# A two-layer decoder trunk with split fp32 weights: slabs of the turned products prepared in pairs

## The chip, the cores and the metric

The kernel runs on one core of a Trainium2 chip. The metric is the device time of one execution in microseconds, as the median of several runs. Busy times, waits and orders come from one profiled execution, whose own time stands beside its span below.

## The reference

```python
DEPTH = 2; D_MODEL = 2048; SEQ = 256; D_FF = 5632; CONV_WIDTH = 3
for layer in range(DEPTH):
    h = rmsnorm(x, g_mix_pre[layer])
    y = even_mixer(...) if layer % 2 == 0 else odd_mixer(...)   # h @ w_in -> q, k, v -> attention -> @ w_out
    x = x + rmsnorm(y, g_mix_post[layer])
    h = rmsnorm(x, g_mem_pre[layer])
    y = memory_cross_attention(h, rmsnorm(mem, g_mem_kv[layer]), wq, wk, wv, wo)
    x = x + rmsnorm(y, g_mem_post[layer])
    h = rmsnorm(x, g_ffn_pre[layer])
    y = conv_ffn(h, w_up[layer], conv_w[layer], conv_b[layer], w_down[layer])
    x = x + rmsnorm(y, g_ffn_post[layer])

def conv_ffn(h, w_up, conv_w, conv_b, w_down):
    u = h @ w_up                                   # (256, 2048) @ (2048, 2 * 5632)
    u = conv_b + conv_w[0]*up[:, 0:S] + conv_w[1]*up[:, 1:S+1] + conv_w[2]*up[:, 2:S+2]
    g, val = u[..., :D_FF], u[..., D_FF:]
    return (silu(g) * val) @ w_down
```

Everything is float32. The weight products (`h @ w_in`, `h @ w_up` and so on) are nearly all of the work.

## The kernel before

**Split weights.** A weight matrix comes in slabs: 256 rows by 512 columns, which on chip is 128 partitions by 1024 elements (two k-tiles of 512 columns), 512 KB. SyncE loads slab n into `raw[:, n % 8]` (`slab`, L529 to L537). ScalarE rounds it to its high part, `w_hi[:, n % 4] = raw` (`split`, L636 to L642). VectorE then writes the low part, `w_lo = raw - w_hi` (L1350 to L1354); `w_lo` lies in the same memory as `raw`, so the low part overwrites the slab in place. TensorE multiplies with both parts. The activations are split in the same way into `a_hi` and `a_lo`, which stand side by side in `a_hl`.

**Four counters order this.** `raw_landed[s]` says that a slot's load has landed, `hi_ready` and `lo_ready` count high and low parts, and `slab_used` counts the slabs that TensorE has finished. SyncE issues slab n once `slab_used` is at least n - 7, ScalarE overwrites a slot of `w_hi` once `slab_used` is at least n - 3, and TensorE starts slab n once `lo_ready` is at least n + 1.

**Turned slabs.** In the query and key groups (groups 1 to 7 of each layer) and in all but the first group of `up`, TensorE keeps the weights stationary (`slab_turned`, L2319 to L2349). A slab then has 8 "wide" products with the high part (L2331; 512 columns, `a_hi` and `a_lo` together) and 8 "narrow" ones with the low part (L2339; 256 columns). Even slabs go wide then narrow, odd slabs narrow then wide, so TensorE changes between the two kinds once per slab. A group is 8 slabs (GS) into four PSUM banks.

**Who runs ahead.** ScalarE and VectorE each have one queue with an order written out by hand. In step s of a group they do that step's other work and then call `ahead`, which splits slab n + 2. The step's other work in `up` belongs to the group that was just finished. For a "val" group, with q counted from the start of the group that follows it: q = 0 ScalarE copies half of each bank to `u_val` (L1200), q = 1 VectorE adds the other half (L2020), q = 2 VectorE scales (L2027), q = 3 ScalarE does the first tap of the convolution in four instructions (L1215) and VectorE the other two taps in eight (L2037, L2045), q = 4 VectorE multiplies by the gate (L2068), q = 5 the result is split too (L1235, L2087). For a "gate" group it is the same from q = 8 to q = 11, with the SiLU at q = 12 (L1223). A pair of groups, 16 slabs, is one turn of `up_pair`. Turns 1 to 4 are written out; turns 5 to 10 are a loop (`Fori`), where the values that are waited for come from registers. Turn 0 has its own first half.

```python
def ahead(n, s=None):
    ...
    split(n + AHEAD, (n + AHEAD) % RAW if s is None else (s + AHEAD) % RAW)   # AHEAD = 2
```

Of the kernel before, what the change touches and what calls it, by code (L numbers as in the profile page):

```python
# [30 lines left out]
F32 = mybir.dt.float32  # L31
F32R = mybir.dt.float32r
I32 = mybir.dt.int32
ALU = mybir.AluOpType
# [3 lines left out]
P = 128  # L38
D = 2048
SEQ = 256  # L40
# [8 lines left out]
N = 512  # L49
# [94 lines left out]
def build(nc, x, mem, positions, w_in_ab, w_out_ab, w_in_c, b_f, w_out_c,  # L144
# [6 lines left out]
    with ctx:  # L151
# [273 lines left out]


        def pair_heads(q):

            return (2 * q, 2 * q + 1) if 0 <= q < HEADS // 2 else ()
# [98 lines left out]
        def _(sp):  # L528
            def slab(n, s, src):  # L529
# [15 lines left out]
            def groups_loop(n0, w, count, col0, stride, slabs, pair=1):  # L545

                with sp.Fori(0, count) as i:
                    for g in range(pair):
                        for s in range(slabs):
                            k = g * slabs + s  # L550
                            slab(i * (pair * slabs) + (n0 + k), k % RAW,
                                 w[s * SLAB_KT * P:(s + 1) * SLAB_KT * P, bass.ds(i * stride + (col0 + g * N), N)])

            sp.dma_start(raw[:, 0, 0, :], w_in_ab[0][0:P, 0:N]).then_inc(first_w[0], 16)
            w_ins, w_outs = (w_in_ab[0], w_in_c[0]), (w_out_ab[0], w_out_c[0])
            for L in range(LAYERS):
# [54 lines left out]
                with sp.Fori(0, FF_GROUPS) as i:  # L611
                    for g in range(2):
                        for s in range(GS):
                            k = g * GS + s
                            slab(i * (2 * GS) + (n0 + PHASE["up"] + k), k % RAW,
                                 w_up[L][s * SLAB_KT * P:(s + 1) * SLAB_KT * P, bass.ds(i * N + g * D_FF, N)])
                for k, (q, g, _) in enumerate(DOWN):
# [17 lines left out]
        def _(act):  # L635
            def split(n, s):  # L636


                act.wait_ge(raw_landed[s], landed(n, s))
                if not (isinstance(n, int) and n < RING):  # L640
                    act.wait_ge(slab_used, n - (RING - 1))
                act.activation(w_hi[:, s % RING], raw[:, s], ACT.Copy).then_inc(hi_ready, 1)  # L642

            def landed(n, s):
                if isinstance(n, int):
                    return landed_ahead[s] + 16 * (n // RAW + 1)
# [153 lines left out]
            for L in range(LAYERS):  # L800
# [63 lines left out]
                def qk_group(G, par, n):  # L864

                    turned = G != 1
                    for s in range(GS):
                        if s == 0 and turned:
                            qk_copy(G - 1, 1 - par)
# [21 lines left out]
                        mem_step((G - 3) * GS + s)  # L891
                        ahead(n + s, s)

# [455 lines left out]
        def _(dve):  # L1349
            def split(n, s):  # L1350


                dve.wait_ge(hi_ready, n + 1)
                dve.tensor_tensor(w_lo[:, s], raw[:, s], w_hi[:, s % RING].bitcast(F32), ALU.subtract).then_inc(lo_ready, 1)  # L1354

            def ahead(n, s=None):
# [154 lines left out]
            for L in range(LAYERS):  # L1511
# [99 lines left out]
                def qk_group(G, par, n):  # L1611
                    turned = G != 1
                    for s in range(GS):
                        if s == 0 and not turned:
                            qk_evac(G - 1, 1 - par)
# [15 lines left out]
                        mem_step((G - 3) * GS + s)  # L1631
                        ahead(n + s, s)

# [457 lines left out]
                def up_pair(i, n, first):  # L2091
                    for q in range(GS if first else 0, 2 * GS):
                        if not first:
                            val_tail(i - 1, q)
# [11 lines left out]
                        if q == GS + (4 if first else 3):  # L2106
                            conv_taps(i * 2, u_turned if first else lambda j: u_gate[:, j, :], conv_gate, 0, i)
                        ahead(n + q, q)

# [179 lines left out]
        def _(pe):  # L2289
# [31 lines left out]
            def slab_turned(n, slot, par, k0):  # L2321
# [27 lines left out]
                last.then_inc(slab_used, 1)  # L2349

            def transposes(dst, src, tiles, done):

# [93 lines left out]
            for L in range(LAYERS):  # L2446
# [58 lines left out]
                def qk_group_turned(G, par, n):  # L2505
                    qk_free(G)
                    for s in range(GS):
# [8 lines left out]
                        if L and G == 5 and s == 0:  # L2516
                            pe.wait_ge(*LV(L, "fg_st", 5))
                        slab_turned(n + s, s % RAW, par, SLAB_KT * s)

# [281 lines left out]
                def up_pair(i, n, first):  # L2801
                    for q in range(GS if first else 0, 2 * GS):
# [4 lines left out]
                        if first and q == GS + 3:  # L2807
                            u_turn()
                        slab_turned(n + q, q % RAW, q // GS, SLAB_KT * (q % GS))

# [126 lines left out]
```

## Time and profile before

| What | Value |
|---|---|
| Median of 3 runs | 2434.69 us (2433.88 to 2435.66) |
| Profiled execution, its own time | 2432.51 us |
| Span of the profiled execution | 2430.7 us |
| TensorE busy | 2415.9 us, 99% of the span |
| VectorE busy | 1855.5 us, 76% |
| ScalarE busy | 1369.8 us, 56% |
| GpSimd busy | 61.7 us, 3% |
| Mean TensorE clock granted | 0.999 of full speed |
| DMA | 477.85 MB, 197 GB/s over the span |

The own time is 1.8 us over the span, which runs from the first to the last instruction. TensorE's matmuls overlap in the records (each is shown longer than the distance to the next), so a busy share of 99% says that TensorE had nearly no gaps, and its pace is read from the distance between starts.

### The profile page before, as it was taken

How to read it: one execution, taken by the hardware profiler on the slowest of the kernel's cores; microseconds unless marked ns; L12 is line 12 of the kernel's file. 1: busy time of each engine (PE TensorE's matmuls, PEld its weight loads, DVE VectorE, ACT ScalarE, POOL GpSimd, SP SyncE). 2: the span in 40 equal slices, each digit the busy share in tenths (PEclk: the TensorE clock that was granted, in tenths of full speed). 3: DMA queues.
4: the chain of work that ended last, by engine and by line, in shares of the span. 5: the costliest groups of instructions: out<-in, count | busy, mean ns of one | idle time of the engine just before them, and what ended most of it. 6: DMA issues, size and time to landing. Idle time of an engine off the chain costs nothing.

```text
span 2430.7 us, 34866 instructions
## 1 busy us (share of the span) xinstructions
PE 2415.9 (99%) x12548; PEld 2067.8 (85%) x12548; DVE 1855.5 (76%) x2559; ACT 1369.8 (56%) x1960; POOL 61.7 (3%) x108
## 2 busy tenths in 40 slices
PE   9999999999999999999999999999999999999998
PEld 7888888888888888888888888888888888888887
DVE  7768877677777677888876588776776776778887
ACT  6545665665555555555555456656655555555554
POOL 0100000000000000000000003000000000000000
PEclk9999999999999999999999999999999999999999
DMA  8766556576666666666776665565666666666665
GB/s 309 250 196 202 163 161 188 164 217 190 190 191 188 187 188 189 208 207 210 228 209 184 191 202 184 164 188 172 210 190 190 191 189 187 187 189 212 203 214 184
DMA packets 252094, 477.85 MB, mean 197 GB/s; under 512 B 18256, under 2 KB 21472, under 8 KB 251968
## 3 DMA queue, kind: packets, MB, share of 16 engines
q1 hardware_dynamic: 234640, 447.83, 60.7%
q10 hardware_dynamic: 17328, 28.35, 3.7%
q8 instruction: 79, 1.29, 0.2%
q14 instruction: 47, 0.39, 0.1%
HBM read 468.89 MB, written 6.31 MB: 195 GB/s over the span
## 4 chain that ended last, share of the span: by engine, by line
PE 94%; DVE 2%; ACT 1%; DMA 1%; issue 1%; POOL 0%; ACTq 0%; POOLq 0%; DVEq 0%
PE acc L2331 17%; PE aux L2331 9%; PE acc L2339 9%; PE tp L2331 8%; PE acc L2310 7%; PE acc L2312 7%; PE acc L2311 7%; PE acc L2304 5%; PE acc L2306 5%; PE acc L2305 5%; PE aux L2339 5%; PE tp L2339 4%; PE tp L2310 1%; DVE w_lo L1354 1%; PE aux L2310 1%; PE aux L2312 1%
## 5 line engine op out<-in xcount | busy, mean ns | idle before, releaser
L1354 DVE TENSOR_TENSOR w_lo<-raw,w_hi 128x1024 fp32r<-128x1024 f32 x847 | 1016.8, 1222 | 425.3 <-ACT w_hi L642 422.6
L642 ACT ACTIVATE w_hi<-raw 128x1024 fp32r<-128x1024 f32 x847 | 867.2, 1054 | 363.4 <-DVE raw L2130 99.9
L2331 PE MATMUL acc<-a_hl,w_hi 128*128 128x512 f32 x1792 | 556.1, 392 | 0.9 <-DVE rope_sin L1568 0.9
L2331 PEld LDWEIGHTS acc<-a_hl,w_hi 128*128 128x128 f32 x1792 | 322.0, 189 | 55.4 <-issue 1.5
L2339 PE MATMUL acc<-a_hl,w_lo 128*128 128x256 f32 x1792 | 360.1, 283 | 0.5 <-DVE w_lo L1354 0.5
L2339 PEld LDWEIGHTS acc<-a_hl,w_lo 128*128 128x128 f32 x1792 | 293.6, 191 | 18.2 <-DVE w_lo L1354 0.8
L2331 PE MATMUL aux<-a_hl,w_hi 128*128 128x512 f32 x960 | 296.4, 390 | 0.0
L2331 PE MATMUL tp<-a_hl,w_hi 128*128 128x512 f32 x832 | 257.0, 390 | 0.0
L2331 PEld LDWEIGHTS aux<-a_hl,w_hi 128*128 128x128 f32 x960 | 180.2, 188 | 39.3
L2339 PE MATMUL aux<-a_hl,w_lo 128*128 128x256 f32 x960 | 193.4, 283 | 0.0
L2304 PE MATMUL acc<-w_hi,a_hl 128*128 128x512 f32 x476 | 191.1, 402 | 1.9 <-DVE a_hl L1383 1.1
L2306 PE MATMUL acc<-w_hi,a_hl 128*128 128x512 f32 x476 | 186.1, 391 | 0.0
L2305 PE MATMUL acc<-w_lo,a_hl 128*128 128x512 f32 x476 | 185.5, 390 | 0.0
L2331 PEld LDWEIGHTS tp<-a_hl,w_hi 128*128 128x128 f32 x832 | 156.2, 188 | 34.1
L2312 PE MATMUL acc<-w_hi,hid_lo 128*128 128x512 f32 x448 | 174.3, 389 | 0.0
L2339 PE MATMUL tp<-a_hl,w_lo 128*128 128x256 f32 x832 | 167.6, 283 | 0.0
L2310 PE MATMUL acc<-w_hi,hid_hi 128*128 128x512 f32 x416 | 161.8, 389 | 0.0
L2311 PE MATMUL acc<-w_lo,hid_hi 128*128 128x512 f32 x416 | 161.8, 389 | 0.0
L2339 PEld LDWEIGHTS aux<-a_hl,w_lo 128*128 128x128 f32 x960 | 149.3, 191 | 0.0
L2339 PEld LDWEIGHTS tp<-a_hl,w_lo 128*128 128x128 f32 x832 | 129.4, 191 | 0.0
L2304 PEld LDWEIGHTS acc<-w_hi,a_hl 128*128 128x128 f32 x476 | 89.4, 188 | 20.7 <-issue 2.0
L2306 PEld LDWEIGHTS acc<-w_hi,a_hl 128*128 128x128 f32 x476 | 89.3, 188 | 19.5
(382 smaller groups left out, 3266.8 us busy)
## 6 DMA issues: line engine op xcount, KB each, us to landing
raw<-in_w_up SPq DMA_DIRECT2D x352, 512.0 KB, 3.7
raw<-in_w_down SPq DMA_DIRECT2D x176, 512.0 KB, 4.6
raw<-in_w_in_c SPq DMA_DIRECT2D x96, 512.0 KB, 3.8
raw<-in_w_in_ab SPq DMA_DIRECT2D x95, 512.0 KB, 3.9
raw<-in_w_out_ab SPq DMA_DIRECT2D x32, 512.0 KB, 3.7
raw<-in_w_out_c SPq DMA_DIRECT2D x32, 512.0 KB, 3.7
raw<-in_w_mk SPq DMA_DIRECT2D x16, 512.0 KB, 4.7
raw<-in_w_mq SPq DMA_DIRECT2D x16, 512.0 KB, 4.2
```

Source lines behind the costliest of these rows:

```text
L642: act.activation(w_hi[:, s % RING], raw[:, s], ACT.Copy).then_inc(hi_ready, 1)
L1354: dve.tensor_tensor(w_lo[:, s], raw[:, s], w_hi[:, s % RING].bitcast(F32), ALU.subtract).then_inc(lo_ready, 1)
L2304: pe.matmul(o, hi[:, kt, rows], w_hi[:, slot % RING, j, :], start=(kt == 0), stop=False)
L2305: pe.matmul(o, hi[:, kt, rows], w_lo[:, slot, j, :], start=False, stop=False)
L2306: return pe.matmul(o, lo[:, kt, rows], w_hi[:, slot % RING, j, :], start=False, stop=(kt == kts - 1))
L2310: pe.matmul(o, a_h, b_h, start=first, stop=False)
L2311: pe.matmul(o, a_h, b_l, start=False, stop=False)
L2312: return pe.matmul(o, a_l, b_h, start=False, stop=last)
L2331: last = pe.matmul(bank, w_hi[:, slot % RING, j, f * P:(f + 1) * P], both, start=(kt == 0), stop=(kt == KT - 1))
L2339: last = pe.matmul(bank[:, SEQ:2 * SEQ], w_lo[:, slot, j, f * P:(f + 1) * P], a_hi[:, kt, :], start=False, stop=False)
```

## The change

Steps of turned groups other than group 1 of the projections and the first turn of `up` now work on two slabs at a time. ScalarE and VectorE call `two_ahead` at the start of every even step, in place of `ahead` at the end of each step: it waits until both slabs of the next pair have landed, and splits them with one instruction of 2048 elements on each engine. ScalarE's wait now also has a condition on `lo_ready`, since `slab_used` is now raised after a slab's wide products, which in every second pair come before its narrow ones. TensorE takes two slabs together in `two_slabs_turned`: one pair goes wide, wide, narrow, narrow, the next narrow, narrow, wide, wide. SyncE issues slab n of these phases once `slab_used` is at least n - 5, where it was n - 7. One more wait is added for TensorE before the forget gate's products of layer 1 (`qk_sum`, 6).

```diff
+        def in_twos(n, up):
+            if not isinstance(n, int):
+                return up
+            at = (n - RAW) % LAYER_SLABS
+            return 2 * GS <= at < 8 * GS or PHASE["up"] + 2 * GS <= at < PHASE["down"]
@@ SyncE: slab
-                    sp.wait_ge(slab_used, n - (RAW - 1))
+                    sp.wait_ge(slab_used, n - (RAW - 1) + (2 if in_twos(n, up) else 0))
@@ ScalarE: split, two_ahead
                     act.wait_ge(slab_used, n - (RING - 1))
+                    if in_twos(n + RING, True):
+                        act.wait_ge(lo_ready, n - (RING - 1))
+            def two_ahead(n, s):
+                m, s = n + AHEAD, (s + AHEAD) % RAW
+                for i in range(2):
+                    act.wait_ge(raw_landed[s + i], landed(m + i, s + i))
+                act.wait_ge(slab_used, m + 1 - (RING - 1))
+                act.wait_ge(lo_ready, m + 1 - (RING - 1))
+                act.activation(w_hi[:, s % RING:s % RING + 2], raw[:, s:s + 2], ACT.Copy).then_inc(hi_ready, 2)
@@ ScalarE and VectorE: up_pair (qk_group likewise)
                     for q in range(GS if first else 0, 2 * GS):
+                        if not first and q % 2 == 0:
+                            two_ahead(n + q, q)
                         if not first:
                             val_tail(i - 1, q)
...
-                        ahead(n + q, q)
+                        if first:
+                            ahead(n + q, q)
@@ VectorE: two_ahead
+                m, s = n + AHEAD, (s + AHEAD) % RAW
+                dve.wait_ge(hi_ready, m + 2)
+                dve.tensor_tensor(w_lo[:, s:s + 2], raw[:, s:s + 2], w_hi[:, s % RING:s % RING + 2].bitcast(F32), ALU.subtract)\
+                    .then_inc(lo_ready, 2)
@@ TensorE
+            def two_slabs_turned(n, slot, par, k0):
...
+                wide_first = (k0 // SLAB_KT) % 4 == 0
+                for part in (0, 1):
+                    for i in range(2):
+                        if (part == 0) == wide_first:
+                            if wide_first:
+                                pe.wait_ge(hi_ready, n + i + 1)
+                            wide(i)
+                        else:
+                            pe.wait_ge(lo_ready, n + i + 1)
+                            narrow(i)
@@ TensorE: forget_gate
+                    pe.wait_ge(*LV(L, "qk_sum", 6))
```

In `wide(i)` the last product of slab i raises `slab_used` by 1.

On VectorE, in layer 0's `up`, written-out turn 1, from the last `ahead` of turn 0 to the product with the gate. Before:

```order
489 L1354 TENSOR_TENSOR w_lo<-raw,w_hi 128x1024 x5
490 L2020 TENSOR_TENSOR u_val<-acc,u_val 128x512
491 L2020 TENSOR_TENSOR u_val<-aux,u_val 128x512
492 L1354 TENSOR_TENSOR w_lo<-raw,w_hi 128x1024
493 L2027 TENSOR_TENSOR u_val<-u_val,rstd_row 128x1024
494 L1354 TENSOR_TENSOR w_lo<-raw,w_hi 128x1024
495 L2037 SCALAR_TENSOR_TENSOR conv_val<-u_val,convT,conv_val 128x255 x4
496 L2045 SCALAR_TENSOR_TENSOR conv_val<-u_val,convT,conv_val 128x254 x4
497 L1354 TENSOR_TENSOR w_lo<-raw,w_hi 128x1024
498 L2068 TENSOR_TENSOR conv_val<-conv_gate,conv_val 128x1024
```

Now:

```order
491 L1378 TENSOR_TENSOR w_lo<-raw,w_hi 128x1024 x4
492 L1384 TENSOR_TENSOR w_lo<-raw,w_hi 128x2048
493 L2054 TENSOR_TENSOR u_val<-acc,u_val 128x512
494 L2054 TENSOR_TENSOR u_val<-aux,u_val 128x512
495 L1384 TENSOR_TENSOR w_lo<-raw,w_hi 128x2048
496 L2061 TENSOR_TENSOR u_val<-u_val,rstd_row 128x1024
497 L2071 SCALAR_TENSOR_TENSOR conv_val<-u_val,convT,conv_val 128x255 x4
498 L2079 SCALAR_TENSOR_TENSOR conv_val<-u_val,convT,conv_val 128x254 x4
499 L1384 TENSOR_TENSOR w_lo<-raw,w_hi 128x2048
500 L2102 TENSOR_TENSOR conv_val<-conv_gate,conv_val 128x1024
```

The scaling of `u_val` now stands behind a low part for two slabs, and the low part for the pair after that stands behind all eight taps.

On ScalarE, the same place. Before:

```order
356 L1200 ACTIVATE u_val<-acc 128x512
357 L1200 ACTIVATE u_val<-aux 128x512
358 L642 ACTIVATE w_hi<-raw 128x1024 x3
359 L1215 ACTIVATE conv_val<-u_val,convT 128x256 x4
360 L642 ACTIVATE w_hi<-raw 128x1024 x2
```

Now:

```order
347 L665 ACTIVATE w_hi<-raw 128x2048
348 L1221 ACTIVATE u_val<-acc 128x512
349 L1221 ACTIVATE u_val<-aux 128x512
350 L665 ACTIVATE w_hi<-raw 128x2048
351 L1236 ACTIVATE conv_val<-u_val,convT 128x256 x4
352 L665 ACTIVATE w_hi<-raw 128x2048
```

Five high parts of one slab around the taps have become three of two slabs, the first of them ahead of the copies, and the third still stands behind the four taps.

## Rows read from the trace of the kernel before

**Rows 1.** The page, its first part: busy us, share of the span, instructions.

```profile
PE 2415.9 (99%) x12548; PEld 2067.8 (85%) x12548; DVE 1855.5 (76%) x2559; ACT 1369.8 (56%) x1960; POOL 61.7 (3%) x108
```

**Rows 2.** Waits of TensorE: us in total, times, longest; the row on a low part.

```profile
PE acc L2339 <- DVE w_lo L1354: 0.5, 1, 0.5
```

**Rows 3.** TensorE's timeline in the `up` loop, narrow to wide: start, us, instruction, count.

```profile
2003.08 0.63 PE L2331 MATMUL acc<-a_hl,w_hi 128*128 128x512 f32 x2
2003.55 0.62 PE L2331 MATMUL aux<-a_hl,w_hi 128*128 128x512 f32 x2
...
2005.38 0.61 PE L2331 MATMUL aux<-a_hl,w_hi 128*128 128x512 f32 x2
2005.83 0.62 PE L2331 MATMUL acc<-a_hl,w_hi 128*128 128x512 f32 x2
```

**Rows 4.** Groups by line: busy us, mean ns, then idle before.

```profile
L1354 DVE TENSOR_TENSOR w_lo<-raw,w_hi 128x1024 fp32r<-128x1024 f32 x847 | 1016.8, 1222 | 425.3 <-ACT w_hi L642 422.6
L642 ACT ACTIVATE w_hi<-raw 128x1024 fp32r<-128x1024 f32 x847 | 867.2, 1054 | 363.4 <-DVE raw L2130 99.9 <-PE acc L2312 67.0 <-PE aux L2331 54.8
...
L2141 DVE TENSOR_TENSOR t_lo<-t_sum,t_hi 128x1536 fp32r<-128x1536 f32 x32 | 56.0, 1752 | 0.3
...
L1304 ACT ACTIVATE t_hi<-t_sum 128x1536 fp32r<-128x1536 f32 x32 | 47.6, 1488 | 10.9 <-DVE t_sum L2135 10.9
```

**Rows 5.** Timeline of the loop, where a val group ends and a gate group starts.

```profile
1971.81 0.60 ACT L1200 ACTIVATE u_val<-acc 128x512 f32<-128x512 f32 x1 [4.59 <-PE aux L2331]
...
2016.06 0.61 PE L2331 MATMUL acc<-a_hl,w_hi 128*128 128x512 f32 x2
...
2016.34 0.60 ACT L1200 ACTIVATE u_val<-acc 128x512 f32<-128x512 f32 x1 [4.59 <-PE aux L2331]
2016.38 0.37 SPq L537 DMA_DIRECT2D raw<-in_w_up  x1
```

**Rows 6.** Timeline of the same turn of the loop, scale and taps.

```profile
2021.88 1.22 DVE L2027 TENSOR_TENSOR u_val<-u_val,rstd_row 128x1024 f32<-128x1024 f32 x1
...
2023.41 2.08 ACT L1215 ACTIVATE conv_val<-u_val,convT 128x256 f32<-128x256 f32 x4 [3.15 <-DVE u_val L2027]
...
2024.67 1.86 DVE L2037 SCALAR_TENSOR_TENSOR conv_val<-u_val,convT,conv_val 128x255 f32<-128x255 f32 x4 [0.43 <-ACT conv_val L1215]
...
2028.02 1.22 DVE L1354 TENSOR_TENSOR w_lo<-raw,w_hi 128x1024 fp32r<-128x1024 f32 x1
```

**Rows 7.** Timeline of a written-out turn, scale and taps.

```profile
1799.13 1.22 DVE L2027 TENSOR_TENSOR u_val<-u_val,rstd_row 128x1024 f32<-128x1024 f32 x1
1800.26 1.22 DVE L1354 TENSOR_TENSOR w_lo<-raw,w_hi 128x1024 fp32r<-128x1024 f32 x1
...
1800.38 2.08 ACT L1215 ACTIVATE conv_val<-u_val,convT 128x256 f32<-128x256 f32 x4 [2.87 <-DVE u_val L2027]
...
1801.51 1.87 DVE L2037 SCALAR_TENSOR_TENSOR conv_val<-u_val,convT,conv_val 128x255 f32<-128x255 f32 x4
...
1804.87 1.22 DVE L1354 TENSOR_TENSOR w_lo<-raw,w_hi 128x1024 fp32r<-128x1024 f32 x1
```

**Rows 8.** Loads of slabs (L537), 1950 to 2040 us, 32 loads: us from issue.

```profile
DMA to landing us min/median/max: 3.5/3.7/4.2
```

**Rows 9.** Two loads 1.6 us apart after a pause: 1218 to 1221, 494 to 496 us.

```profile
L537 SPq DMA_DIRECT2D raw<-in_w_in_c x2: 379/379/379, 1218.8 to 1220.4; - x2
...
DMA to landing us min/median/max: 3.6/4.0/4.3
...
L537 SPq DMA_DIRECT2D raw<-in_w_up x2: 373/373/373, 494.0 to 495.7; - x2
...
DMA to landing us min/median/max: 3.7/4.5/5.2
```

**Rows 10.** Timeline of one of the two places where TensorE waits for VectorE among turned slabs.

```profile
54.28 0.40 DVE L1568 COPY rope_sin<-acc 32x256 f32<-32x256 f32 x1
...
54.94 0.70 PE L2331 MATMUL acc<-a_hl,w_hi 128*128 128x512 f32 x2 [0.86 <-DVE rope_sin L1568]
```

More of the change, by code:

```diff
@@ L528, in _, with slab @@
         def _(sp):
-            def slab(n, s, src):
+            def slab(n, s, src, up=False):
                 if isinstance(n, int) and n < RAW:
@@ L867, in qk_group @@
                     for s in range(GS):
+                        if turned and s % 2 == 0:
+                            two_ahead(n + s, s)
                         if s == 0 and turned:
@@ L891, in qk_group @@
                         mem_step((G - 3) * GS + s)
-                        ahead(n + s, s)
+                        if not turned:
+                            ahead(n + s, s)
                 def v_blocks_hi(z):
@@ L1354, in split, with two_ahead @@
                 dve.tensor_tensor(w_lo[:, s], raw[:, s], w_hi[:, s % RING].bitcast(F32), ALU.subtract).then_inc(lo_ready, 1)
+            def two_ahead(n, s):
+                m, s = n + AHEAD, (s + AHEAD) % RAW
+                dve.wait_ge(hi_ready, m + 2)
+                dve.tensor_tensor(w_lo[:, s:s + 2], raw[:, s:s + 2], w_hi[:, s % RING:s % RING + 2].bitcast(F32), ALU.subtract)\
+                    .then_inc(lo_ready, 2)
             def ahead(n, s=None):
@@ L1613, in qk_group @@
                     for s in range(GS):
+                        if turned and s % 2 == 0:
+                            two_ahead(n + s, s)
                         if s == 0 and not turned:
@@ L1631, in qk_group @@
                         mem_step((G - 3) * GS + s)
-                        ahead(n + s, s)
+                        if not turned:
+                            ahead(n + s, s)
                 def first_group(n):
@@ L2092, in up_pair @@
                     for q in range(GS if first else 0, 2 * GS):
+                        if not first and q % 2 == 0:
+                            two_ahead(n + q, q)
                         if not first:
@@ L2107, in up_pair @@
                             conv_taps(i * 2, u_turned if first else lambda j: u_gate[:, j, :], conv_gate, 0, i)
-                        ahead(n + q, q)
+                        if first:
+                            ahead(n + q, q)
                 up_pair(0, n, True)
@@ L2349, in slab_turned, with wide, narrow @@
                 last.then_inc(slab_used, 1)
+            def two_slabs_turned(n, slot, par, k0):
+                def wide(i):
+                    for j in range(SLAB_KT):
+                        kt = k0 + SLAB_KT * i + j
+                        both = a_hl[:, kt].rearrange("p a b -> p (a b)")
+                        for f, bank in enumerate(u_banks(par)):
+                            last = pe.matmul(bank, w_hi[:, (slot + i) % RING, j, f * P:(f + 1) * P], both, start=(kt == 0),
+                                             stop=(kt == KT - 1))
+                    last.then_inc(slab_used, 1)
+                def narrow(i):
+                    for j in range(SLAB_KT):
+                        kt = k0 + SLAB_KT * i + j
+                        for f, bank in enumerate(u_banks(par)):
+                            pe.matmul(bank[:, SEQ:2 * SEQ], w_lo[:, slot + i, j, f * P:(f + 1) * P], a_hi[:, kt, :],
+                                      start=False, stop=False)
+                wide_first = (k0 // SLAB_KT) % 4 == 0
[8 more added lines that the diff above has]
+                            narrow(i)
             def transposes(dst, src, tiles, done):
@@ L2808, in up_pair @@
                             u_turn()
-                        slab_turned(n + q, q % RAW, q // GS, SLAB_KT * (q % GS))
+                        if first:
+                            slab_turned(n + q, q % RAW, q // GS, SLAB_KT * (q % GS))
+                        elif q % 2 == 0:
+                            two_slabs_turned(n + q, q % RAW, q // GS, SLAB_KT * (q % GS))
                 up_pair(0, n, True)
```

9 lines of the change are left out of this document (6 added, 3 removed).

## The prediction, blind

> **What bounds the kernel now.** I read the page's busy times first. TensorE is busy 99% of the span [rows 1], VectorE 76% and ScalarE 56%: cheaper work on those two shortens nothing by itself, unless TensorE waits for it. The waits of TensorE come next: among all turned slabs it waits once for a low part, 0.5 us [rows 2]. So TensorE's own pace sets the end, and a change to who prepares slabs can win almost nothing there. It can lose, if a low part comes late. The sum is therefore made on two questions: what does TensorE itself save, and does every pair of slabs arrive in time. For the second the timeline of one turn of `up` is needed, on all engines.
>
> **How many.** Pairs are used in groups 2 to 7 of both layers (6 x 4 x 2 = 48) and in ten turns of `up` per layer (10 x 8 x 2 = 160): 208 pairs in place of 416 single slabs.
>
> **ScalarE and VectorE work, taken away and hidden.** A low part of 1024 elements takes 1.222 us, a subtraction of 1536 takes 1.752 [rows 4], so 512 elements cost 0.53 and a pair's 2048 should take 2.28. On ScalarE 1.054 and 1.488 give 1.92. VectorE saves 208 x (2.44 - 2.28) = 33 us and ScalarE 208 x (2.11 - 1.92) = 39 us of busy time, under a TensorE without gaps: worth 0 in time. The Trainium skill ("VectorE: DVE Perf Modes", the TRN2 errata section) says that operations on SBUF pay a fixed latency per instruction and advises larger tiles; the rows agree, and read as a rule for this change it would promise those 33 us. The sum takes none of it, because VectorE isn't what ends last [rows 1].
>
> **TensorE, saved.** After narrow products the first wide ones are slower: two of them take 0.47 us (2003.08 to 2003.55) where later two take 0.45 (2005.38 to 2005.83) [rows 3]. Over the six pairs of products between 2003.08 and 2005.83 that is 2.75 against 6 x 0.454 = 2.72, about 0.02 to 0.03 per change of kind. Each slab had one change within it, and half of these 416, 208, led from narrow to wide; 104 are left. 104 x 0.02 = **-2 us**. Bounds: 0 (the slow start belongs to something else) and -3. More waits stand in TensorE's queue in a wide-first pair (two on high parts beside two on low parts); nothing shows a price for a wait that is met, so 0, at most what the saving is.
>
> **The hand-off, the term that decides.** Call t = 0 the start of a group's first product. A slab takes 44.53 / 16 = 2.78 us (1971.81 to 2016.34, 16 slabs) [rows 5], a pair 5.57. The pair that matters is the fourth of a group, narrow-first, starting at t = 3 x 5.57 = 16.70: its low parts must be complete then. In the changed order of VectorE they stand behind the eight taps, those behind ScalarE's first tap, that behind the scaling, and the scaling behind the low parts of the third pair. The chain, for the second half of a turn in the loop and alike for the first:
>
> - The third pair is slabs 4 and 5 of the group. SyncE may issue slab n once slab n - 6 is used, so slab 5 goes out when the last slab before the group is done, at t = 0.32 (2016.38 against 2016.06) [rows 5]. Before, it was issued two slabs earlier.
> - It lands L later. With even spacing of 2.78 us L is 3.7 [rows 8]. But releases now come in bursts: in a narrow-first pair the two wide parts end 1.8 us apart, at the pair's end, then a wide-first pair gives two more 1.8 us apart at its start, and then 5.6 us pass. The load in question is the second of such four. Two loads 1.6 us apart after a pause occur five times in the trace, and the second lands after 4.3, 4.5, 4.7, 4.9 and 5.2 us; the lowest and the highest are in [rows 9]. Between 4.7 at 1.6 and 3.7 at 2.78, spacing 1.8 gives L = 4.5. Ends: 3.7 and 5.2.
> - ScalarE's `two_ahead` waits for both loads and has two more waits behind. The price of two such waits isn't in a row by itself. The scaling's end to the first tap is 0.31 us in the loop (2023.10 to 2023.41) [rows 6] and 0.03 in a written-out turn (1800.35 to 1800.38) [rows 7]. I take 0.20 in the loop and 0.05 outside, ends 0 and 0.3.
> - High part 1.92, hand-over 0.03, low part 2.19 to the next start (2.28 less the 0.09 by which neighbours overlap: 1.22 long, 1.13 apart [rows 7]).
> - From the scaling's start to the taps' start on VectorE: 2.79 in the loop (2021.88 to 2024.67) [rows 6], 2.38 outside (1799.13 to 1801.51) [rows 7]. Taps to the next low part: 3.35 and 3.36.
> - Low part of the fourth pair 2.28. From the end of VectorE's work to TensorE's start: 0.26 (54.68 to 54.94) [rows 10].
>
> Loop: 0.32 + 4.50 + 0.20 + 1.92 + 0.03 + 2.19 + 2.79 + 3.35 + 2.28 + 0.26 = 17.84, which is 1.14 late. Written out: 0.32 + 4.50 + 0.05 + 1.92 + 0.03 + 2.19 + 2.38 + 3.36 + 2.28 + 0.26 = 17.29, 0.59 late. Each half of a turn starts a chain of its own from its own t = 0, so the delays add up: 6 turns x 2 halves x 2 layers = 24 in the loops, 4 x 2 x 2 = 16 outside. 24 x 1.14 + 16 x 0.59 = 27.4 + 9.4 = **+37 us**. Behind the late low part VectorE has the gate product, and ScalarE the split of the result; both have over one pair of slack.
>
> **Other pairs, at nothing.** The second pair is narrow-first like the fourth, but no taps stand ahead of it. Its high part starts when the pair before the group is released, 0.28 us after t = 0 [rows 5], and 0.28 + 1.92 + 0.03 + 2.28 + 0.26 is 4.8 of the 5.57 us there are: cover 0.8 us. If that goes, the copies and sums of a finished group are late next, and they have a whole group. Wide-first pairs need only high parts at once; their low parts have 3.6 us more. In the query and key groups the scaling or rotation isn't followed by taps, so the chain is over 3 us shorter: 0. The copies of a group now stand behind a 1.9 us high part on ScalarE; the banks they free are wanted one group (22 us) later: 0. The blocks for `down` in turns 1 and 2 fit between the third and fourth pair's work by some 0.3 us: 0. TensorE's new wait before the forget gate is on a sum three steps old: 0. SyncE's later issue delays nobody else in its queue but the next slabs, counted above.
>
> **The sum.** 2432.5 + 37 - 2 = 2467.5 us for an execution like the profiled one. That one lies 2.2 us under the median of the runs, so I predict **2469 us**.
>
> **Rivals.**
> *A, the forecast:* the fourth pair is late by 0.6 to 1.2 us in each half, 2450 to 2489 as L goes from 4.0 to 5.1. For it: every term but L and the two waits has its row. Against it: the chain has ten links, and 0.1 us less in each would undo it.
> *B, loads land as with even spacing.* L = 3.7: loop 0.34 late, written out -0.21, that is nothing. 24 x 0.34 - 2 = +6: 2441, or 2437 if the two waits cost nothing. For it: the mean rate of loads is unchanged. Against it: all five second loads in [rows 9] and like them. The Trainium skill ("SBUF — State Buffer", the DMA setup-cost knee) fits a transfer as 2 us plus its bytes at 436 GB/s, 3.2 us for 512 KB, the same for each load; by that the loads are never what ScalarE waits for, and the time would be about 2437. The trace has 3.7 for a load alone, so it doesn't agree.
> *C, no delay and a cheaper TensorE, the other side.* Place: the changes of kind and the waits of TensorE. Price: -2 us by the sum; to show as faster, each of the 104 removed changes must be worth 0.05 us, a -5, and no chain may be late. It decides once L is at or under 3.4 us in the loop, since 1.14 must go. 2428 to 2433. Against it: no load in [rows 8] is under 3.5.
> *D, more is late than the one chain.* With L over 5.1, or the second pair of each group late too, another 0.5 us x 40: 2490 to 2510.
> *E, it doesn't do what it says.* The order on both engines shows the 2048-element operations, so this has no share worth naming.
>
> **How the numbers follow.** About 0.2% or 4.9 us is what a measurement of this kernel can tell from no change. A 0.65, B 0.18, C 0.09, D 0.08. A and D are slower. Of B, L of 3.7 gives +6 or +2, so half is slower and half is the same. C's own sum of -2 is within 0.2%; only a third to a half of it is faster. That makes faster 0.04, same 0.14, slower 0.82. The range reaches from the middle of B, 2439, to the top of A, 2489, and leaves out C, half of B and most of D, about 2 in 10.
>
> **What would show it.** The waits of TensorE should have one new large row, narrow products waiting for a 2048-element `w_lo`, about 40 times, with 0.6 us in written-out turns and 1.1 in loops, always in the fourth pair of a group in `up` and not in the query and key groups. VectorE's `w_lo` of 2048 should take 2.28 us and ScalarE's `w_hi` 1.92. Median landing of `up` should rise from 3.7 to over 4.2. VectorE's busy time should fall by some 33 us. In narrow-first pairs the wait for `w_hi` should be ended by a load. I am wrong if TensorE's idle time stays as it is (then a link is shorter, and the L line tells whether it is the load), or if waits of size show at other pairs.

## The result and the profile after

The changed kernel took 2484.22 us (median of 6 runs, 2478.94 to 2490.6), the kernel before 2435.11 us beside it (6 runs, 2433.88 to 2436.89). The ratio is 1.020 [1.019, 1.021]: slower by 49 us. The forecast was 2469, its range 2439 to 2489. The profiled execution of the changed kernel took 2484.21 us, span 2482.4, granted clock 0.998; against the 2432.51 of the profiled execution before, that is 51.7 us to account for.

The page's busy times of the changed kernel, which answer to [rows 1]:

```profile
PE 2428.8 (98%) x12548; PEld 2074.8 (84%) x12548; DVE 1844.1 (74%) x2351; ACT 1349.1 (54%) x1752; POOL 63.5 (3%) x108
```

VectorE and ScalarE are less busy, by 11 and 21 us, and the kernel is slower. The waits of TensorE say where (us in total, times, longest):

```profile
PE acc L2404 <- DVE w_lo L1384: 38.3, 39, 2.5
PE acc L2341 <- DVE a_hl L1414: 1.5, 1, 1.5
```

L2404 is the narrow product of `two_slabs_turned`, L1384 the 2048-element low part of `two_ahead`. One new row has taken the place of the 0.5 us of [rows 2]. The page's chain of what ended last agrees:

```profile
PE 66%; DVE 12%; DMA 9%; ACT 6%; issue 5%; ACTq 1%; DVEq 0%; POOL 0%; SPq 0%; POOLq 0%
```

Here 12% stands for VectorE, 9% for DMA and 6% for ScalarE, in a kernel whose chain was 94% TensorE before: these are the links of the hand-off. Groups by line, which answer to [rows 4] (busy us, mean ns, idle before):

```profile
L1384 DVE TENSOR_TENSOR w_lo<-raw,w_hi 128x2048 fp32r<-128x2048 f32 x208 | 476.4, 2290 | 307.7 <-ACT w_hi L665 307.5
...
L665 ACT ACTIVATE w_hi<-raw 128x2048 fp32r<-128x2048 f32 x208 | 397.4, 1911 | 365.3 <-PE aux L2396 136.5
```

The sizes are those of the forecast: 2.29 and 1.91 us for 2.28 and 1.92. The loads (L544) between 800 and 1000 us, which answer to [rows 8], where the median was 3.7:

```profile
DMA to landing us min/median/max: 3.5/4.5/5.0
```

**One late pair, link by link.** This is the timeline of the first half of a loop turn in layer 0. Its group starts at t = 0 = 822.07. One fence for each engine, SyncE, ScalarE, VectorE and TensorE:

```profile
822.39 0.37 SPq L544 DMA_DIRECT2D raw<-in_w_up  x1
```

```profile
827.40 1.92 ACT L665 ACTIVATE w_hi<-raw 128x2048 fp32r<-128x2048 f32 x1 [2.09 <-DMA raw<-in_w_up]
833.09 2.08 ACT L1236 ACTIVATE conv_val<-u_val,convT 128x256 f32<-128x256 f32 x4 [3.77 <-DVE u_val L2061]
```

```profile
829.42 2.29 DVE L1384 TENSOR_TENSOR w_lo<-raw,w_hi 128x2048 fp32r<-128x2048 f32 x1 [1.49 <-ACT w_hi L665]
831.63 1.22 DVE L2061 TENSOR_TENSOR u_val<-u_val,rstd_row 128x1024 f32<-128x1024 f32 x1
834.34 1.85 DVE L2071 SCALAR_TENSOR_TENSOR conv_val<-u_val,convT,conv_val 128x255 f32<-128x255 f32 x4 [1.49 <-ACT conv_val L1236]
836.12 1.66 DVE L2079 SCALAR_TENSOR_TENSOR conv_val<-u_val,convT,conv_val 128x254 f32<-128x254 f32 x4
837.69 2.28 DVE L1384 TENSOR_TENSOR w_lo<-raw,w_hi 128x2048 fp32r<-128x2048 f32 x1
```

```profile
822.07 0.62 PE L2396 MATMUL acc<-a_hl,w_hi 128*128 128x512 f32 x2
...
838.48 0.40 PE L2404 MATMUL tp<-a_hl,w_lo 128*128 128x256 f32 x2
840.03 0.51 PE L2404 MATMUL acc<-a_hl,w_lo 128*128 128x256 f32 x2 [1.15 <-DVE w_lo L1384]
840.37 0.40 PE L2404 MATMUL tp<-a_hl,w_lo 128*128 128x256 f32 x2
```

Read it downwards. The second load of the third pair goes out at t = 0.32 and lands 4.8 us later. ScalarE stood idle 2.09 us for it. The low part of that pair ends at 831.71, the scaling of `u_val` has waited behind it, ScalarE's tap has waited for the scaling, and VectorE's taps for ScalarE's. The low part of the fourth pair ends at 839.97. Two narrow products are 0.24 us apart, so the one at 840.03 was due at 838.72: 1.31 us late. The two after it start 0.34 later, 0.10 more than the usual distance.

The same chain can be read at all 38 late pairs of `up`, and only one of its links varies. The second load of the third pair lands between 4.15 and 5.67 us after its issue. Every other link stays within 0.09 us in the loops and within 0.02 in the written-out turns. So each delay follows the landing one for one: it is the landing less 3.87 us in the 14 written-out halves, and the landing less 3.38 to 3.47 in the 24 of the loops.

### The profile page after: what moved, and what is told of

The parts are those of the page before. It is cut to its first block, busy times and chain, and to the rows that moved or that the text cites. A ratio compares the mean times of both kernels' runs of the same rounds, so it can differ in the third digit from the quotient of the medians.

```text
span 2482.4 us, 34611 instructions
## 1 busy us (share of the span) xinstructions
PE 2428.8 (98%) x12548; PEld 2074.8 (84%) x12548; DVE 1844.1 (74%) x2351; ACT 1349.1 (54%) x1752; POOL 63.5 (3%) x108
## 4 chain that ended last, share of the span: by engine, by line
PE 66%; DVE 12%; DMA 9%; ACT 6%; issue 5%; ACTq 1%; DVEq 0%; POOL 0%; SPq 0%; POOLq 0%
DMA raw<-in_w_up 7%; PE acc L2396 7%; PE acc L2347 6%; PE acc L2349 6%; PE acc L2348 6%; DVE w_lo L1384 5%; PE acc L2341 5%; PE acc L2343 5%; PE acc L2342 5%; PE acc L2404 4%; PE tp L2396 3%; PE aux L2396 3%; ACT w_hi L665 3%; PE tp L2404 2%; PE aux L2404 2%
## 5 line engine op out<-in xcount | busy, mean ns | idle before, releaser
L1384 DVE TENSOR_TENSOR w_lo<-raw,w_hi 128x2048 fp32r<-128x2048 f32 x208 | 476.4, 2290 | 307.7 <-ACT w_hi L665 307.5
L1378 DVE TENSOR_TENSOR w_lo<-raw,w_hi 128x1024 fp32r<-128x1024 f32 x431 | 516.7, 1223 | 112.1 <-ACT w_hi L651 109.5
L665 ACT ACTIVATE w_hi<-raw 128x2048 fp32r<-128x2048 f32 x208 | 397.4, 1911 | 365.3 <-PE aux L2396 136.5
L651 ACT ACTIVATE w_hi<-raw 128x1024 fp32r<-128x1024 f32 x431 | 448.9, 1055 | 251.7 <-DVE raw L2167 100.1
L2396 PE MATMUL acc<-a_hl,w_hi 128*128 128x512 f32 x1664 | 515.4, 391 | 0.9 <-DVE rope_sin L1599 0.9
L2404 PE MATMUL acc<-a_hl,w_lo 128*128 128x256 f32 x1664 | 339.5, 286 | 38.4 <-DVE w_lo L1384 38.3
L2404 PEld LDWEIGHTS acc<-a_hl,w_lo 128*128 128x128 f32 x1664 | 266.4, 192 | 54.7 <-DVE w_lo L1384 46.6
L2396 PE MATMUL aux<-a_hl,w_hi 128*128 128x512 f32 x832 | 257.0, 390 | 0.0
L2396 PEld LDWEIGHTS aux<-a_hl,w_hi 128*128 128x128 f32 x832 | 156.5, 188 | 33.4
L2404 PE MATMUL tp<-a_hl,w_lo 128*128 128x256 f32 x832 | 168.3, 284 | 0.0
L2404 PE MATMUL aux<-a_hl,w_lo 128*128 128x256 f32 x832 | 167.9, 283 | 0.0
L2404 PEld LDWEIGHTS tp<-a_hl,w_lo 128*128 128x128 f32 x832 | 130.2, 193 | 0.0
L2404 PEld LDWEIGHTS aux<-a_hl,w_lo 128*128 128x128 f32 x832 | 129.8, 192 | 0.0
```

The costliest lines, as they stand in the source:

```text
L665: act.activation(w_hi[:, s % RING:s % RING + 2], raw[:, s:s + 2], ACT.Copy).then_inc(hi_ready, 2)
L1384: dve.tensor_tensor(w_lo[:, s:s + 2], raw[:, s:s + 2], w_hi[:, s % RING:s % RING + 2].bitcast(F32), ALU.subtract)\
L2396: last = pe.matmul(bank, w_hi[:, (slot + i) % RING, j, f * P:(f + 1) * P], both, start=(kt == 0), stop=(kt == KT - 1))
L2404: pe.matmul(bank[:, SEQ:2 * SEQ], w_lo[:, slot + i, j, f * P:(f + 1) * P], a_hi[:, kt, :], start=False, stop=False)
```

## The experiments

For how late each pair is, I took the distances between the starts of neighbouring narrow products, normally 0.12 us each, and summed what is over that wherever a distance is 0.20 or more ("late" below). The changed kernel has 51.0 us of it, the kernel before 0.6.

The theory (A) is the chain above: a load that lands late in a burst, whose 2048-element high and low part stand ahead of the scaling, whose taps stand ahead of the next low part. Each of the first experiments cuts one link of it and leaves the rest of the change in place.

**1. The scaling ahead of the low part.**

```diff
@@ VectorE: val_tail
-                    if q == 2:
-                        u_scale(i * 2 + 1, u_val)
...
@@ VectorE: up_pair
+                        if not first and q == 2:
+                            u_scale((i - 1) * 2 + 1, u_val)
...
                         if not first and q % 2 == 0:
                             two_ahead(n + q, q)
```

The gate group's scaling (q == GS + 2) moves in the same way, and the last val group's goes ahead of the steps of `down`.

> The changed kernel, but VectorE does the scaling of a finished up group ahead of the low parts of the third pair, not behind them. Nothing is left out. Theory A (the fourth pair is late by a chain: second load of the third pair, high parts, low parts, scaling, first tap, eight taps, low parts): the scaling starts at about t = 5.9 instead of 9, the taps end before the fourth pair's high parts are there (13.3), its low parts end at 15.6 and TensorE needs them at 16.4. The waits of TensorE for low parts in up go from 46 us to under 2; what stays is 4 us in the query and key groups of layer 0. Time 2434 to 2440. Theory B (pairs cost TensorE itself something, in waits or in the order of products): nothing changes, 2479 to 2490. Theory C (the operations of 2048 elements are what is late, wherever they stand): at least half of the delay stays, over 2458.

Measured: 2434.93 us (10 runs), ratio 1.0004 [0.9995, 1.0014], as theory A had it. TensorE's wait, and the second half of a loop turn on both engines:

```profile
PE acc L2406 <- DVE w_lo L1384: 2.2, 2, 1.6
```

```profile
836.29 1.92 ACT L665 ACTIVATE w_hi<-raw 128x2048 fp32r<-128x2048 f32 x1 [2.27 <-DMA raw<-in_w_up]
838.15 2.08 ACT L1236 ACTIVATE conv_gate<-u_gate,convT 128x256 f32<-128x256 f32 x4
```

```profile
836.68 1.23 DVE L2061 TENSOR_TENSOR u_gate<-u_gate,rstd_row 128x1024 f32<-128x1024 f32 x1
838.31 2.29 DVE L1384 TENSOR_TENSOR w_lo<-raw,w_hi 128x2048 fp32r<-128x2048 f32 x1 [0.41 <-ACT w_hi L665]
```

The load is still late (2.27 us of idle on ScalarE), the 2048-element operations and TensorE's pairs are as in the changed kernel, and the delay is gone: the scaling now runs while ScalarE makes the high part. From the high part's start to VectorE's first tap, which now comes right behind the low part, it is 4.23 us (836.29 to 840.52); in the example above the taps began 6.94 us after it. One exchange of two instructions on VectorE takes back all 49 us.

**2. Pairs in order and in TensorE, but each part of two operations.**

```diff
@@ ScalarE and VectorE: two_ahead
-                act.activation(w_hi[:, s % RING:s % RING + 2], raw[:, s:s + 2], ACT.Copy).then_inc(hi_ready, 2)
+                for i in range(2):
+                    act.activation(w_hi[:, (s + i) % RING], raw[:, s + i], ACT.Copy).then_inc(hi_ready, 1)
...
-                dve.wait_ge(hi_ready, m + 2)
-                dve.tensor_tensor(w_lo[:, s:s + 2], raw[:, s:s + 2], w_hi[:, s % RING:s % RING + 2].bitcast(F32), ALU.subtract)\
-                    .then_inc(lo_ready, 2)
+                for i in range(2):
+                    dve.wait_ge(hi_ready, m + i + 1)
+                    dve.tensor_tensor(w_lo[:, s + i], raw[:, s + i], w_hi[:, (s + i) % RING].bitcast(F32), ALU.subtract)\
+                        .then_inc(lo_ready, 1)
```

> The changed kernel, with the same waits for both loads and the same places in both queues, but each instruction of 2048 elements is two of 1024, on ScalarE and on VectorE, each with its own count. Nothing is left out. Theory A: VectorE's first low part of the third pair starts 0.9 us sooner and the chain behind it moves up by 0.8; TensorE's first narrow product of the fourth pair needs only one slab's low part, another 1.1 us. 1.9 us less than a delay of 1.0 to 1.3: none is left in most halves. Time 2433 to 2440, though VectorE and ScalarE work some 30 us more. Theory B (TensorE's pairs themselves): 2479 to 2490. A theory D, that only the late load matters and not the length of the instructions: the load is as late as before, so over 2475.

Measured: 2434.61 us (10 runs), ratio 1.0004 [0.9994, 1.0014], again as theory A had it. Waits of TensorE, then VectorE and ScalarE in a loop turn:

```profile
PE acc L2406 <- DVE w_lo L1386: 1.1, 2, 0.7
```

```profile
789.96 2.36 DVE L1386 TENSOR_TENSOR w_lo<-raw,w_hi 128x1024 fp32r<-128x1024 f32 x2 [1.39 <-ACT w_hi L666]
792.24 1.22 DVE L2063 TENSOR_TENSOR u_gate<-u_gate,rstd_row 128x1024 f32<-128x1024 f32 x1
```

```profile
788.87 2.01 ACT L666 ACTIVATE w_hi<-raw 128x1024 fp32r<-128x1024 f32 x2 [1.97 <-DMA raw<-in_w_up]
```

ScalarE's high parts start at 788.87 and VectorE's low parts at 789.96, 1.09 us later. In the changed kernel it was 827.40 and 829.42, 2.02 us. So the two engines overlap within the pair, and the chain is 0.86 us shorter (0.93 by the start of the low parts, less 0.07, since two of them take 2.36 us and not 2.29). At its end TensorE may start when the first low part of the fourth pair is done, after 1.22 us and not 2.28. Together that is 1.9 us, more than the 1.3 us that a pair of the loops was late on average. Two operations cost more busy time and are 49 us better.

**3. The loads earlier, nothing else changed.** Of each four slabs the first three may now go out at the same count of `slab_used`, and the fourth one release later.

```diff
-                    sp.wait_ge(slab_used, n - (RAW - 1) + (2 if in_twos(n, up) else 0))
+                    sp.wait_ge(slab_used, n - (RAW - 1) + ((2, 1, 0, 0)[s % 4] if in_twos(n, up) else 0))
```

> The changed kernel with its order and its 2048-element instructions, and only the loads as early as their slots are free. Nothing is left out. The third pair's second slab is issued together with its first, 1.3 us sooner than in the changed kernel, but right behind it, with a third load behind. Theory A: the chain moves up by what the landing gains. Loads 0.5 us apart are in the trace of before only at the kernel's start and land later than 4.7; with 5.3 after 1.36 us of spacing the landing would be at about 4.3 to 5.0 instead of 5.0, so 0 to 0.7 us less delay in 40 halves: 2455 to 2484. Theory C (length of the instructions only): 2479 to 2490, no change at all although the load lands sooner. If the landing doesn't move, the run tells nothing between them.

Measured: 2435.6 us (10 runs), ratio 1.0005 [0.9996, 1.0015]. That is a miss, by 20 us: I had expected 2455 to 2484, with between 20 and 49 us of the loss left. ScalarE in a loop turn whose group starts at 785.78, and the loads (L544) of its burst, in two stretches; they are issued at 784.29, 784.85, 785.4 and 786.11:

```profile
789.77 1.92 ACT L665 ACTIVATE w_hi<-raw 128x2048 fp32r<-128x2048 f32 x1 [0.74 <-PE aux L2396]
```

```profile
L544 SPq DMA_DIRECT2D raw<-in_w_up x1: 373/373/373, 784.3 to 784.3; - x1
DMA to landing us min/median/max: 3.9/3.9/3.9
...
L544 SPq DMA_DIRECT2D raw<-in_w_up x2: 373/373/373, 784.8 to 785.4; - x2
DMA to landing us min/median/max: 4.7/5.1/5.5
```

The high part starts 3.99 us after t = 0, where it was 5.33. That is 1.34 earlier, just what the loop's pairs were late. And what ends ScalarE's wait is now TensorE's release of the slot, no load. Loads 0.56 us apart take longer each (4.7, 5.5 and 6.0 us for the second to the fourth), but each only 0.6 to 0.8 us more than the one before. The second is issued 1.25 us earlier than in the changed kernel and takes no longer, 4.7 for 4.8. My expectation had put a price on the crowding, and for the load that counts there is none. In all 3.8 us are late.

**4. The loads later by one more slab.**

```diff
-                    sp.wait_ge(slab_used, n - (RAW - 1) + (2 if in_twos(n, up) else 0))
+                    sp.wait_ge(slab_used, n - (RAW - 1) + (3 if in_twos(n, up) else 0))
```

> The changed kernel, with every load of these phases issued one slab later still (slab_used at least n - 4, where the changed kernel has n - 5). Nothing is left out. Theory A (the third pair's second load starts the chain): its issue moves from t = 0.3 to 2.1, so each of the 40 halves loses about 1.8 us more there, or some less where the second pair is late too and takes part of it; the second pair's load lands at 2.2 where its high parts could start at 0.4, which makes that pair late by about 1.2 us in up and in the query and key groups. Together 80 to 120 us over the changed kernel: 2560 to 2605. A theory E, that loads land in time anyway and the chain starts at the release of the high parts' slots: under 2500.

Measured: 2612.28 us (4 runs), ratio 1.074 [1.070, 1.077]. Waits of TensorE, and of ScalarE:

```profile
PE acc L2404 <- DVE w_lo L1384: 125.7, 98, 2.8
```

```profile
ACT w_hi L665 <- DMA raw<-in_w_up: 263.4, 73, 10.0
```

The sign is that of the theory. The size is 7 us over the expected range, 2560 to 2605, so the theory's price was a little low. The landing is no longer (median of `up` 4.5 us, as in the changed kernel), so it is the time of issue that costs. The mean granted clock was 0.992 for 0.998: the many long stalls cost some clock too, which was not in the expectation.

**5. The pairs on ScalarE and VectorE alone.** TensorE goes slab by slab and SyncE issues as before, n - 7.

```diff
@@ TensorE: turned groups (up_pair likewise)
-                        if G == 1:
-                            slab_turned(n + s, s % RAW, par, SLAB_KT * s)
-                        elif s % 2 == 0:
-                            two_slabs_turned(n + s, s % RAW, par, SLAB_KT * s)
+                        slab_turned(n + s, s % RAW, par, SLAB_KT * s)
@@ SyncE: slab
-                    sp.wait_ge(slab_used, n - (RAW - 1) + (2 if in_twos(n, up) else 0))
+                    sp.wait_ge(slab_used, n - (RAW - 1))
```

> Only ScalarE and VectorE work in pairs; TensorE takes slab by slab and SyncE issues as in the kernel before. Nothing is left out. All loads are early and evenly spaced again. Theory A with its second condition: ScalarE's high parts for two slabs need two free slots, and TensorE now frees the second only at the end of the first pair, at t = 5.9 instead of 3.9 after its wide products; the chain starts at 5.9 instead of 4.6 to 5.3, and the pair after the fourth needs its low parts at its start, another 1 us late. 40 halves with 1.5 to 3 us: 2500 to 2560, slower than the changed kernel. Theory F (only the late loads made the change slow): the waits go away, 2432 to 2445.

Measured: 2527.27 us (4 runs), ratio 1.038 [1.037, 1.040], in the range of theory A. Waits of TensorE:

```profile
PE acc L2368 <- DVE w_lo L1384: 75.1, 62, 1.7
```

Waits of ScalarE, where the changed kernel has 136.5 us in 28 and 89.8 us in 33:

```profile
ACT w_hi L665 <- PE aux L2368: 203.0, 51, 5.4
ACT w_hi L665 <- PE tp L2368: 135.1, 52, 7.3
```

The median landing is at 3.7 us as before the change. The high part waits for TensorE to finish both slabs whose slots of `w_hi` it overwrites, and TensorE gives them up one by one, each at its slab's end. So a 2048-element operation for a consumer that takes and frees single slabs is worse than the changed kernel (2527 for 2484), although its loads go out earlier. With TensorE in pairs and early loads, experiment 3, the same operations cost nothing that can be told (2435.6): the order on TensorE is what makes room for them.

**6. TensorE's pairs and SyncE's wait alone.** ScalarE and VectorE work slab by slab, as before.

```diff
@@ ScalarE and VectorE: up_pair (turned groups likewise)
-                        if not first and q % 2 == 0:
-                            two_ahead(n + q, q)
...
-                        if first:
-                            ahead(n + q, q)
+                        ahead(n + q, q)
```

> The changed kernel with TensorE in pairs and SyncE's later issue, but ScalarE and VectorE split slab by slab at the end of each step, as in the kernel before. Nothing is left out. Theory A: all low parts are in time (the last of the fourth pair just so), and what is left of the change is TensorE's saving, 104 slow starts of wide products less, about 2 us: 2432 to 2438, TensorE's narrow and wide runs with the same pace as in the changed kernel. Theory B (TensorE's pairs and their waits cost): over 2460.

Measured: 2440.29 us (10 runs), ratio 1.0026 [1.0016, 1.0036], 2 us over the expected range and slower than before. Waits of TensorE:

```profile
PE acc L2392 <- DVE w_lo L1372: 3.8, 13, 0.6
```

Late by 9.7 us, at 49 distances. Most of it lies at the last slab of 32 narrow products in a row, the second of the fourth pair. In 17 of the 104 such rows of narrow products its first one starts 0.28 us or more after the one before it, where 0.12 is usual, and in all 12 turns of the loops the distance is 0.51 to 0.59. The timeline of such a turn:

```profile
733.37 1.23 DVE L2112 TENSOR_TENSOR hid_lo<-conv_val,hid_hi 128x1024 f32 x1 [0.22 <-ACT hid_hi L1253]
```

```profile
735.78 0.51 PE L2392 MATMUL acc<-a_hl,w_lo 128*128 128x256 f32 x2 [0.24 <-DVE w_lo L1372]
```

The low part of the slab before starts at 731.93, the one that TensorE waits for only at 734.51, 2.58 us later. Between them stands the split of the finished result (`hid_lo`), which itself waits for ScalarE's `hid_hi`. The kernel before has the same order on VectorE. But there TensorE wanted the last slab's narrow products 2.78 us after it began the slab before, and in a narrow-first pair it wants them after 8 x 0.12 = 0.96 us. I had named this margin in the expectation and taken it as just met. In the changed kernel this low part stands ahead of the gate product and of the split.

**7 and 8. The cures together.** First experiments 1 and 2 in one kernel, then 1, 2 and 3.

The edits are those of 1, 2 and 3 unchanged.

> The changed kernel with both cures: the scaling ahead of the third pair's low parts, and two instructions of 1024 elements instead of one of 2048 on ScalarE and VectorE. Nothing is left out. Theory A: each alone took away the late low parts in up and left 3.4 and 2.1 us late in the query and key groups of layer 0; together nothing more can come from up, and what shows is TensorE's saving of 2 us less what the query and key groups still lose, about 2: 2431 to 2436, the same as before within what can be told. Theory B (pairs cost TensorE itself): over 2438.

> As the run with both cures, and SyncE issues each load as early as its slot is free: slabs of narrow-first pairs at slab_used n - 7 as before the change, the first slab of a wide-first pair at n - 5, the second at n - 6. Nothing is left out. Theory A: the low parts are in time already, so loads that come sooner gain only what the query and key groups of layer 0 lose, up to 2 us: 2430 to 2435. A theory that the late issue itself costs (a fuller DMA at the wrong moment): under 2429.

Measured: 2433.58 us (11 runs), ratio 0.9996 [0.9987, 1.0005], and 2432.79 us (11 runs), ratio 0.9994 [0.9985, 1.0003]. Both lie in their expected ranges, and neither can be told from the kernel before. The busy times of the second, whose span is 2428.3:

```profile
PE 2415.1 (99%) x12548; PEld 2069.8 (85%) x12548; DVE 1852.4 (76%) x2559; ACT 1373.0 (57%) x1960; POOL 61.0 (3%) x108
```

With 0.6 us late in all, as in the kernel before, this one has what the change can give, and that is TensorE's saving: in the changed kernel two pairs take 11.113 us of products (32 wide in a row 7.281, 32 narrow 3.832), where four slabs took 11.132 before. That is 0.019 for each of 104, 2.0 us. The ratio agrees with it and doesn't show it, since its interval takes in 1.

## Why the prediction was right, and where it was short

**The mechanism** held at each link. Experiments 1, 2 and 3 each cut one link and each took back the whole loss; experiment 4 lengthened one and made it worse. Rival B (loads land as with even spacing) falls by the 4.5 us median and by the 38 loads that count, none of which landed in under 4.15 us; rival C falls with it. The fit in the Trainium skill ("SBUF — State Buffer", the DMA setup-cost knee) gives an estimate of 3.2 us for each 512 KB load. The trace disagrees, with 3.5 to 5.0 us in that row, as it did in [rows 8].

**The sum** was +37 - 2 for 24 loop halves and 16 written-out ones; the execution shows +51.7. Term by term:

- *How many.* 38 halves are late, not 40: 24 in the loops, 14 outside. The first half in twos of each layer isn't, since SyncE still issues its third pair by the old rule. (TensorE's wait row has 39 entries, two of them in query groups; it leaves out one of the shortest.)
- *Loop, 1.14 each.* Measured 32.0 us over 24, 1.33 each. In the example: issue 0.32 (as put), landing 4.8 (4.5), load to high part 0.24 (0.20), start of high to start of low part 2.02 (1.95), low part to scaling 2.21 (2.19), scaling to taps 2.71 (2.79), taps 3.35 (3.35), low part 2.28, to TensorE 0.06 (0.26). So the landing was 0.3 too small (its mean over the 24 is 4.78), and the lag to TensorE, taken from a copy of another shape [rows 10], 0.2 too large. These two errors have opposite signs and partly cancel, which was luck.
- *Written out, 0.59 each.* Measured 9.4 us over 14, 0.67 each; the landing is 4.54 on average here. The sum of 9.4, just as forecast, is luck: two halves fewer, each 0.08 later.
- *A late start's own cost, not in the sum.* The first two products after a wait take 0.34 us in place of 0.24: 0.10 x 38 = 3.9 us.
- *The first loop turns.* In each layer one pair is over 2 us late, both in the first turn of the loop. Their part of the 32.0 us is 4.3. The loads (L544) issued at 723.88, 725.69, 727.51 and 729.32 us landed after 3.7, 5.7, 5.2 and 4.7 us, where the burst of the example began with 3.7 and 4.8. The second of them is the load that counts; in layer 1 it took 5.6 us, and these two are the slowest of the 38. Why these bursts are slower I did not test.
- *The clock, not in the sum.* It fell after both of these stalls; the rows are below. From the distances of the products it cost 1.5 us at the one and 1.6 at the other.
- *Query and key groups, taken as 0.* They have 3.3 us in layer 0, in two places, due at 118.6 and 132.5 us. Rows below.
- *TensorE, -2.* Measured -2.0.

The differences, in us: loops +4.6, written out 0, restarts +3.9, clock +3.1, query and key +3.3 and 0.2 for its two restarts, together 15.1 of the 16.7 by which 51.7 exceeds 35. The rest, 1.6 us, is not accounted for; single executions of this kernel differ by up to 12 us.

The step that failed outright is "the chain is over 3 us shorter: 0" for the query and key groups. No taps follow there, that is true. But ScalarE has other work, and VectorE's rotation waits for a DMA that ScalarE issues. ScalarE's timeline in layer 0:

```profile
112.88 0.62 ACT L713 ACTIVATE junk<-mem_in 128x512 f32<-128x512 f32 x1
...
114.84 1.22 ACTq L874 DMA_DIRECT2D swapped<-qkT  x1
116.09 0.61 ACTq L875 DMA_DIRECT2D swapped<-qkT  x1
116.90 1.91 ACT L665 ACTIVATE w_hi<-raw 128x2048 fp32r<-128x2048 f32 x1 [2.56 <-PE tp L2396]
```

```profile
121.26 0.50 PE L2404 MATMUL acc<-a_hl,w_lo 128*128 128x256 f32 x2 [2.46 <-DVE w_lo L1384]
```

From 112.88 to 116.70 us ScalarE squares and sums rows of the memory (L713) and then issues DMAs, 1.8 us for the two of `swapped`, and the high part comes 3.6 us after the release of its slots (113.3 us: 0.28 after the start of a pair 5.6 before 118.65). The low part for two slabs can't start until it ends. The other place hangs on the same two DMAs, on VectorE:

```profile
123.52 1.21 DVE L1609 TENSOR_TENSOR swapped<-swapped,rope_sin 32x1024 f32<-32x1024 f32 x1 [2.31 <-DMA swapped<-qkT]
...
127.87 2.27 DVE L1384 TENSOR_TENSOR w_lo<-raw,w_hi 128x2048 fp32r<-128x2048 f32 x1
130.07 0.86 DVE L1709 SCALAR_TENSOR_TENSOR m_lo<-m_t,gT,m_hi 128x256 fp32r<-128x256 f32 x2
130.86 2.27 DVE L1384 TENSOR_TENSOR w_lo<-raw,w_hi 128x2048 fp32r<-128x2048 f32 x1
```

```profile
133.19 0.50 PE L2404 MATMUL acc<-a_hl,w_lo 128*128 128x256 f32 x2 [0.56 <-DVE w_lo L1384]
```

`swapped` lands some 7 us after its issue, and VectorE stands idle for 2.31 us. Then come the rotation, a low part, other work and the low part that TensorE wants at 132.47; it ends at 133.13. So here the rotation took the part that the taps have in `up`. Both places were read from the traces alone. The late 0 to 560 us are 3.8 us in the changed kernel and 3.0 in experiment 1; they are 1.8 and 2.1 in experiments 2 and 7, whose operations are short, and 1.4 and 0.2 in those with early loads.

**The large operations saved** less busy time than the 33 and 39 us put down for them: VectorE 11.4 and ScalarE 20.7. Two records of 1024 overlap (2.36 and 2.01 us for two in the rows of experiment 2), so against 2.29 and 1.91 they save 208 x 0.07 = 15 and 208 x 0.10 = 21, which is nearer. It mattered nothing, as the forecast said: [rows 1].

## What to carry to other kernels

A merged operation delivers its first half only when its second is done, and its consumer's slots free in the same grain; ask which instruction queues behind it, how late its own input comes, and whether the next deadline has that much slack. Here the merged operations saved 11 and 21 us on two engines with time to spare, and together with the later loads they cost (41.4 + 3.9) / 38 = 1.2 us in each of 38 chains. When such a chain is just too long, one cut is enough, and one that cost nothing here is to put the short instruction that others wait for (the scaling) ahead of the long one that still waits for a load.

## What the runs showed of the hardware

**Loads close together.** The first 512 KB load of a burst landed after 3.7 us in the example of the changed kernel and 3.9 in that of experiment 3. The second landed after 4.8 at 1.8 us distance and 4.7 at 0.56, the third and fourth at 0.56 after 5.5 and 6.0. The four of experiment 3 landed 1.4, 1.3 and 1.3 us apart. I had not expected that a three times closer spacing leaves the second load's time as it is. So a spacing of 1.8 already cost a full microsecond, and for the second load issuing earlier was a gain in full. At the same spacing of 1.8 the time still scatters, from 4.15 to 5.67 us over the 38.

**The clock after a stall.** Stretches of the changed kernel: us, busy times of PE, PEld, DVE, ACT and POOL, the granted clock, DMA share, GB/s.

```profile
741.00:744.00 3.00, 1.18 (x10) 0.97 (x9) 3.00 (x4) 0.18 (x1) 0.00 (x0) 1.00 0.88 325
744.00:749.00 5.00, 4.78 (x22) 4.51 (x23) 3.13 (x4) 2.86 (x2) 0.00 (x0) 0.66 0.01 5
2000.00:2003.00 3.00, 1.06 (x9) 0.86 (x9) 2.83 (x3) 2.34 (x2) 0.00 (x0) 1.00 0.83 303
2003.00:2007.00 4.00, 4.00 (x20) 3.71 (x21) 2.29 (x1) 0.52 (x1) 0.00 (x0) 0.65 0.00 1
909.00:912.00 3.00, 1.60 (x13) 1.40 (x13) 2.20 (x2) 2.62 (x2) 0.00 (x0) 1.00 0.77 287
912.00:914.00 2.00, 2.00 (x15) 1.83 (x14) 2.00 (x1) 0.00 (x0) 0.00 (x0) 1.00 0.00 0
121.30:123.50 2.20, 2.20 (x17) 2.17 (x18) 0.00 (x0) 2.17 (x7) 0.00 (x0) 1.00 0.84 239
```

After the stalls of 2.05 us before 744.23 and 1.94 before 2002.88 TensorE ran with clocks of 0.66 and 0.65 on average over 5 and 4 us, that is in part at 1.2 GHz and not 2.4. Narrow products started 0.21 us apart there in place of 0.12, wide ones 0.43 in place of 0.23. After the 1.4 us of stall at 910 it did not fall, and neither after the 2.46 us at 121. So a stall of 2 us can cost over a microsecond more than itself; what tells 121 from the other two is open.
